# Column-group modulation with its twenty later weight chunks inside the input projection of a two-block diffusion kernel

## Chip, cores and metric

The kernel runs on one NeuronCore of one Trainium2 chip, in one launch. The metric is the device time of an execution in microseconds (us). Before the change the median of 3 runs is 4326.28 us (4324.57 to 4330.62).

## The reference, cut to what matters

Three blocks run one after the other on 512 latent rows and 256 context rows of width 1024 (block 1 is a state-space mixer, block 2 an attention, both with a mixture of experts behind them; block 3 is not touched here). The change concerns the modulation vectors of blocks 1 and 2, and where in the program they are computed.

```python
silu_c, silu_cc = silu(c), silu(c_ctx)                       # (1, 1024) and (1024,)
for i in range(2):
    sh1l, sc1l, g1l, sh2l, sc2l, g2l = split(silu_c  @ ada_w[i] + ada_b[i], 6)   # ada_w[i]: (1024, 6144)
    sh1c, sc1c, g1c, sh2c, sc2c, g2c = split(silu_cc @ ada_w[i] + ada_b[i], 6)
    h_lat = rmsnorm(x, norm1_w[i]) * (1 + sc1l) + sh1l
    h_ctx = rmsnorm(ctx, norm1_w[i]) * (1 + sc1c) + sh1c
    o_ctx, o_lat = ssd_mixer(h_ctx, h_lat, ...) if i == 0 else attn_mixer(h_ctx, h_lat, ...)
    x = x + g1l * o_lat
    x = x + g2l * moe_ec(rmsnorm(x, norm2_w[i]) * (1 + sc2l) + sh2l, ...)
# ssd_mixer begins with u @ in_w (1024 x 6208), a 5-tap convolution over the rows, and silu
```

So each `ada_w[i]` is read once (24 MB in float32) and multiplied by only two rows of conditions.

## The kernel before, in words

**Weights** come through a ring of three slots of 2 MB in SBUF (`Ring`, L72 ff.). The plan of chunks is a list made once in `build`; a chunk is a matrix of 1024 rows by 512 columns as `[128, 8, 512]`. SyncE's queue (SP) issues the loads in order: `load_to(sp, end)` issues every chunk of the plan below `end`, and ahead of chunk k waits until chunk k-3, which has its slot, is used up. A chunk is used up when its last matmul is done, or, where it is cut into two fp32r parts (high and low), when its last block is cut. SP does nothing else meanwhile: its program is one line of waits and issues.

**Stages.** Each function is a block of its own; all engines meet between two of them. In order: `setup` (masks, 20 small loads of parameter rows, their transposes, silu of the conditions), `modulation(0)`, `norm_turn` (row norm, transposes, scale and shift, fp32r parts), `ssd_project` (input projection), `ssd_scan`, `norm_turn`, `project_add`, `moe(0)`, `modulation(1)`, `norm_turn`, `project` (queries, keys, values), `qk_prepare` and the rest of block 2, then block 3.

**`modulation(layer)`** (L378 to L432) takes 12 ring chunks of `ada_w[layer]`. For each, TensorE multiplies the two condition columns (the stationary operand is 128 x 2) by 8 slices of 512 columns in float32 (L405), VectorE adds the bias (L421), and at the end 32 small transposes (L412) turn shifts and scales into per-partition columns `modc`; the rows go to DRAM for the gates.

**`ssd_project`** (L610 ff.) has three parts. GpSimd cuts every block of the weights: a cast to the high part (L127), then a subtraction for the low part (L133); it runs at most four blocks ahead of TensorE's marks.
- z: 4 chunks, each cut into 4 blocks of two k slices. For a block TensorE takes 6 token tiles x 2 k x 3 products of 512 columns (L440). ScalarE applies silu (L740), SP stores the rows (L658). PSUM banks go round by 8.
- dt: one chunk of only 64 columns, then a softplus on VectorE and ScalarE.
- x: 8 chunks, each cut into 4 blocks of 128 features; the 32 feature tiles are numbered f. For one f, TensorE takes 24 products of 512 and 24 of 256 columns, then `turn(f-1)`: 6 transposes (L708) of the feature tile before. ScalarE copies the products into a padded tile (L756), VectorE convolves (L801 and four times L805) and then files the transposes of f-1 (L791, L792), ScalarE applies silu (L763, L764). ScalarE's order is copy f, silu f, copy f+1. SP stores the filed tile.

What sets the order of the loads around the change is this loop of SP (L662 ff.):

```python
for f in range(ft):
    if f % 4 == 0:
        ring.load_to(sp, first + nz + 1 + f // 4 + SLOTS)
    if f >= 16:
        sp.wait_ge(silu, f + 1)
        ...
    if 1 <= f <= 24:
        sp.wait_ge(filed, f)
        ...
```

When SP comes to f = 4j it is thus told to load up to two chunks beyond the one that f = 4j uses. `filed` reaches f when `file(f-1)` is done, and VectorE does that after the convolution of f. `turn(f-1)` has two pairs of PSUM banks in turn, (4, 5) and (6, 7).

Of the kernel before, what the change touches and what calls it, by code (L numbers as in the profile page):

```python
# [289 lines left out]
def setup(env):  # L290

    nc, ins = env.nc, env.ins
    with Stage(env, 0) as st:
# [19 lines left out]
        @block.sync  # L313
        def _(sp):
            sp.wait_ge(masks, 1)
            for src, t, r, k in pieces:
                sp.dma_start(rows[r:r + k, t, :], src).then_inc(loaded, 16)
            sp.dma_start(env.dtb[:], ins["ssd_dt_bias"].rearrange("a b c -> a (b c)")
                         .partition_broadcast(P)).then_inc(loaded, 16)
            env.ring_.load_to(sp, SLOTS)  # L320
            sp.wait_ge(loaded, 16 * (len(pieces) + 1))
# [41 lines left out]
        @block.scalar  # L363
        def _(act):
            act.wait_ge(copied, 1)
# [11 lines left out]
def modulation(env, layer):  # L377


    ps, ring = env.ps, env.ring_  # L380
    n_chunks = 12
    with Stage(env, 0 if layer == 0 else X_END) as st:
        mod = st.sb("mod_rows", [2, 6 * D])
        bias = st.sb("ada_bias", [2, 6 * D])
        bias_in, added, turned, stored = st.sem("bias_in"), st.sem("bias_added"), st.sem("mod_turned"), st.sem("mod_stored")
        first, m0 = ring.take([1] * n_chunks)
        block = st.block()

        @block.sync
        def _(sp):  # L390
            sp.dma_start(bias, env.ins["ada_b"][layer, :].partition_broadcast(2)).then_inc(bias_in, 16)
            ring.load_to(sp, first + n_chunks + SLOTS)
            sp.wait_ge(added, n_chunks)
            sp.dma_start(env.mod_dram[layer, :, :], mod).then_inc(stored, 16)
            sp.wait_ge(stored, 16)

        @block.tensor
        def _(pe):
            for n in range(n_chunks):
                if n >= 4:  # L400
                    pe.wait_ge(added, n - 3)
                ring.wait(pe, first + n)
                w = ring.view(first + n, KD, HALF)
                for k in range(KD):
                    mm = pe.matmul(ps[0:2, n % 4, :], env.cond[:, k, :], w[:, k, :], start=k == 0, stop=k == KD - 1)  # L405
                mm.then_inc(ring.done, 1)
            pe.wait_ge(added, n_chunks)

            for q, piece in enumerate((0, 1, 3, 4)):
                for k in range(KD):  # L410
                    a = piece * D + k * P
                    tr = pe.transpose(ps[:, 4, q * 16 + 2 * k:q * 16 + 2 * k + 2], mod[:, a:a + P], env.ident[0:2, 0:2])  # L412
            tr.then_inc(turned, 1)

        @block.vector
        def _(dve):
            dve.wait_ge(bias_in, 16)
            for n in range(n_chunks):
                dve.wait_ge(ring.done, m0 + n + 1)
                s = slice(n * HALF, (n + 1) * HALF)  # L420
                dve.tensor_tensor(mod[:, s], ps[0:2, n % 4, :], bias[:, s], ALU.add).then_inc(added, 1)  # L421
            dve.wait_ge(turned, 1)
            v = ps[:, 4, 0:64].rearrange("p (q k v) -> p q v k", q=4, k=KD)

            for q in range(4):
                dve.tensor_copy(env.modc[:, q, :, :], v[:, q, :, :])
            dve.drain()
            for q, name in ((1, "norm1_w"), (3, "norm2_w")):
                a = env.col_at[name] + layer * KD
                for u in range(2):  # L430
                    dve.scalar_tensor_tensor(env.modc[:, q, u, :], env.modc[:, q, u, :], 1.0, env.cols[:, a:a + KD],
                                             ALU.add, ALU.mult)  # L432
# [179 lines left out]
def ssd_project(env, t, base):  # L612
# [5 lines left out]
    with Stage(env, base) as st:  # L618
# [20 lines left out]
        blocks, m0, b0 = ring.take_cut([marked(HALF)] * nz + [marked(2 * H)]  # L639
                                       + [[(all_k, slice(f * P, (f + 1) * P), 2) for f in range(4)]] * nx)  # L640
        first = blocks[0][0]
        views = {first + n: ring.view(first + n, KD, 2 * H if n == nz else HALF) for n in range(nz + 1 + nx)}
# [7 lines left out]
        def _(sp):  # L650
            sp.dma_start(alog[:], ins["ssd_A_log"].rearrange("a b c -> a (b c)").partition_broadcast(P)).then_inc(alog_in, 16)

            for n in range(nz):
                ring.load_to(sp, first + n + 1 + SLOTS)
# [4 lines left out]
            for f in range(ft):  # L659
                if f % 4 == 0:  # L660
                    ring.load_to(sp, first + nz + 1 + f // 4 + SLOTS)
# [5 lines left out]
                if 1 <= f <= 24:  # L667
# [5 lines left out]
                                 tm[:, q_ % 2, :].rearrange("p (t c) -> p t c", t=NT)).then_inc(tm_out[q_ % 2], 16)  # L673
            for par in range(2):
# [5 lines left out]
        def _(pe):  # L680
            for n in range(nz + 1):
                wide = HALF if n < nz else 2 * H
                for b in range(4):
# [3 lines left out]
                    for i in range(NT):  # L687
                        g = n * NT + i
                        if g >= 8 and b == 0:
                            pe.wait_ge(out, g - 7)  # L690
                        t_ = slice(i * P, (i + 1) * P)
                        for q in range(2):
                            k = 2 * b + q
                            mm = products(pe, ps[:, g % 8, 0:wide], (t.hh[:, k, t_], t.hl[:, k, t_]),
                                          (hi[:, q, :], lo[:, q, :]), k == 0, k == KD - 1)
# [2229 lines left out]
```

## Time and profile before

| What | us |
|---|---|
| median of 3 runs | 4326.28 |
| the profiled execution, its own time | 4335.98 |
| span of its instructions | 4334.2 |
| TensorE busy in it | 3661.4 |
| mean granted TensorE clock (1 is 2.4 GHz) | 0.894 |
| first and last start of the matmuls of L405 | 18.5 and 1929.7 |

The profile is of one execution. Times of instructions are given from the start of the span. Records of matmuls overlap, since the array is pipelined; how fast they follow one another is read from the starts. A float32 matmul appears as two records. "Idle before" is the time an engine stood still ahead of an instruction, with what ended it. PEld is the loading of stationary operands, SPq the issuing of loads and stores by SP.

### The profile page before, as it was taken

The numbers are of one execution on the slowest core, as the hardware profiler recorded it, in microseconds if no ns is written. First come the engines' busy times: TensorE is split into PE (matmuls) and PEld (weight loads), VectorE is DVE, ScalarE is ACT, GpSimd is POOL, SyncE is SP. The second block draws the span as 40 slices with busy tenths as digits, with TensorE's granted clock in tenths as the row PEclk, the third lists the DMA queues.
The fourth block names the chain that finished last, engine by engine and source line by source line (L and its number), as shares of the span: only waits on it lengthen the run. The fifth ranks groups of instructions, "written<-read, shape, count | busy, mean of one in ns | idle before, by whom it ended". The sixth has DMA issues, their size and how long they took to land. (4 is left out here: it accounts for less than half of the span.)

```text
span 4334.2 us, 44977 instructions
## 1 busy us (share of the span) xinstructions
PE 3661.4 (84%) x17353; PEld 2613.0 (60%) x17353; DVE 2334.1 (54%) x2935; ACT 1655.1 (38%) x2498; POOL 1495.3 (34%) x714
## 2 busy tenths in 40 slices
PE   8699979967969999888497899996943999577997
PEld 1588869963456666516366455554832666456876
DVE  0108856662169999811764999994068311213410
ACT  0211223322037777602252677774222311343222
POOL 0333323540056666502003566663300122123432
PEclk9889999988969999988798899997965599798998
DMA  8222343332079999861003899993100022122230
GB/s 283 77 102 72 124 155 98 98 127 97 11 290 381 383 386 383 313 240 41 1 1 139 323 378 377 379 378 129 57 24 0 10 88 93 58 73 88 79 125 34
DMA packets 300449, 703.78 MB, mean 162 GB/s; under 512 B 15688, under 2 KB 62628, under 8 KB 297156
## 3 DMA queue, kind: packets, MB, share of 16 engines
q1 hardware_dynamic: 294092, 679.93, 42.6%
q0 software_dynamic: 6144, 20.98, 2.3%
q8 instruction: 138, 2.26, 0.2%
q14 instruction: 75, 0.61, 0.0%
HBM read 653.59 MB, written 47.28 MB: 162 GB/s over the span
## 5 line engine op out<-in xcount | busy, mean ns | idle before, releaser
L133 POOL TENSOR_TENSOR weights_low<-ring,weights_high 128x1024 fp32r<-128x1024 f32 (+2 forms) x210 | 493.0, 2352 | 1352.9 <-ACT weights_high L126 1345.5
L440 PE MATMUL ps<-h_parts,weights_high 128*128 128x512 f32 (+2 forms) x2528 | 741.1, 379 | 30.8 <-POOL weights_low L133 30.5
L440 PEld LDWEIGHTS ps<-h_parts,weights_high 128*128 128x128 f32 (+1 forms) x2528 | 464.0, 191 | 126.3 <-POOL weights_low L133 31.5
L440 PE MATMUL ps<-h_parts,weights_low 128*128 128x512 f32 (+2 forms) x1264 | 475.3, 376 | 0.0
L1548 DVE TENSOR_TENSOR more_low<-area,more_high 128x1024 fp32r<-128x1024 f32 x192 | 330.4, 1759 | 0.0
L1515 ACT ACTIVATE weights_high<-ring 128x1024 fp32r<-128x1024 f32 x256 | 271.3, 1061 | 136.4 <-PE ps L1448 93.5
L1515 ACT ACTIVATE more_high<-area 128x1024 fp32r<-128x1024 f32 x256 | 271.8, 1062 | 85.8 <-PE ps L1448 85.8
L1548 DVE TENSOR_TENSOR weights_low<-ring,weights_high 128x1024 fp32r<-128x1024 f32 x192 | 300.1, 1616 | 2.7 <-ACT weights_high L1515 2.7
L1419 POOL TENSOR_TENSOR more_low<-area,more_high 128x1024 fp32r<-128x1024 f32 x64 | 242.7, 3792 | 110.7 <-ACT more_high L1515 110.7
L440 PE MATMUL ps<-weights_high,h_parts 128*128 128x512 f32 (+2 forms) x832 | 250.8, 385 | 21.8 <-POOL weights_low L133 21.8
L440 PEld LDWEIGHTS ps<-h_parts,weights_low 128*128 128x128 f32 (+1 forms) x1264 | 240.9, 191 | 46.6
L126 ACT ACTIVATE weights_high<-ring 128x1024 fp32r<-128x1024 f32 (+1 forms) x158 | 161.8, 1040 | 279.7 <-PE ps L440 230.3
L587 PE MATMUL ps<-identity,area 128*128 128x128 f32 x304 | 51.3, 345 | 207.6 <-DVE area L556 137.4
L1419 POOL TENSOR_TENSOR weights_low<-ring,weights_high 128x1024 fp32r<-128x1024 f32 x64 | 168.0, 2625 | 110.8 <-ACT weights_high L1515 110.8
L1446 PE MATMUL ps<-weights_high,gathered_high 128*96 128x512 f32 (+1 forms) x512 | 203.7, 398 | 2.9 <-DVE gathered_low L1554 2.9
L1447 PE MATMUL ps<-weights_low,gathered_high 128*96 128x512 f32 (+1 forms) x512 | 204.3, 399 | 0.0
L1448 PE MATMUL ps<-weights_high,gathered_low 128*96 128x512 f32 (+1 forms) x512 | 203.3, 397 | 0.0
L1446 PE MATMUL ps<-more_high,gathered_high 128*96 128x512 f32 (+1 forms) x512 | 202.8, 396 | 0.0
L1448 PE MATMUL ps<-more_high,gathered_low 128*96 128x512 f32 (+1 forms) x512 | 201.5, 394 | 0.0
L1447 PE MATMUL ps<-more_low,gathered_high 128*96 128x512 f32 (+1 forms) x512 | 201.1, 393 | 0.0
L440 PEld LDWEIGHTS ps<-weights_high,h_parts 128*128 128x128 f32 x832 | 167.6, 215 | 50.0 <-POOL weights_low L133 22.3
L405 PE MATMUL ps<-ring,conditions 128*2 128x512 f32 x384 | 170.8, 608 | 22.9 <-PEq L249 18.2
(408 smaller groups left out, 7545.9 us busy)
## 6 DMA issues: line engine op xcount, KB each, us to landing
ring<-in_moe_w SPq DMA_DIRECT2D x96, 2048.0 KB, 10.7
area<-in_moe_w SPq DMA_DIRECT2D x96, 2048.0 KB, 10.3
ring<-in_ada_w SPq DMA_DIRECT2D x24, 2048.0 KB, 7.8
ring<-in_ssd_in_w SPq DMA_DIRECT2D x12, 2048.0 KB, 8.6
ring<-in_w_in SPq DMA_DIRECT2D x11, 2048.0 KB, 7.7
ring<-in_w_ffn_in SPq DMA_DIRECT2D x10, 2048.0 KB, 7.8
area<-x_dram SPq DMA_DIRECT2D x18, 1024.0 KB, 5.0
ring<-in_ssd_out_w SPq DMA_DIRECT2D x4, 2048.0 KB, 8.6
```

The source lines that it names most:

```text
L126: return eng.activation(hi, src, ACT.Copy)
L133: pool.tensor_tensor(lo, views[k][:, ks, cols], hi, ALU.subtract).then_inc(self.low_p, 1)
L405: mm = pe.matmul(ps[0:2, n % 4, :], env.cond[:, k, :], w[:, k, :], start=k == 0, stop=k == KD - 1)
L440: mm = pe.matmul(out, a, b, start=start and n == 0, stop=stop and n == 2)
L587: tr = pe.transpose(ps[:, n % 8, j * P:(j + 1) * P], xn[:, first - t0 + j, k * P:(k + 1) * P], env.ident[:])
L1419: pool.tensor_tensor(lo(m), raw(m), hi(m), ALU.subtract).then_inc(low_p, 1)
L1446: pe.matmul(out, a, h, start=first, stop=False)
L1447: pe.matmul(out, a, l, start=False, stop=False)
L1448: return pe.matmul(out, b, h, start=False, stop=last)
L1515: act.activation(hi(m), raw(m), ACT.Copy).then_inc(high, 1)
L1548: dve.tensor_tensor(lo(m), raw(m), hi(m), ALU.subtract).then_inc(low_v, 1)
```

## The change

A class `Modulate` replaces `modulation`. It pads the two condition columns to 32 (30 zero columns), and lets the 8 k slices of a chunk go to four column groups of the array, `k % 4`: four partial sums stand in partitions 0, 32, 64 and 96 of one PSUM bank (`products`). ScalarE copies the bank to SBUF (`copy`), a float32 matmul with a matrix of ones and zeros adds the four up (`sums`), VectorE adds the bias (`add`), four small transposes (`turn`) and a copy (`file`) make the columns.

Of the 24 chunks, 4 (shift and scale of the first norm of block 1) are used in a new stage `prologue`, which also has the work of the first `norm_turn`. The other 20 are used in `ssd_project`: numbers 0 to 4 behind the z and dt chunks, numbers 5 to 19 in its x part, products in even f and sums in odd f. In the plan, two of them follow each x chunk. `modulation(1)` is gone. Rows go to banks 6 and 7, so z uses six banks and `turn(f-1)` one pair. The parameter rows are loaded from ScalarE's queue, and the rows of x and the first ring chunk by SP from the start.

```diff
@@ setup
-            sp.wait_ge(masks, 1)
-            for src, t, r, k in pieces:
-                sp.dma_start(rows[r:r + k, t, :], src).then_inc(loaded, 16)
...
+            env.ring_.load_to(sp, 1)
+            for i, s in enumerate(env.xin):
+                sp.dma_start(env.x0[:, i, :], s).then_inc(env.x0_in, 16)
             env.ring_.load_to(sp, SLOTS)
...
+            act.wait_ge(masks, 1)
+            for src, t, r, k in pieces:
+                act.dma_start(rows[r:r + k, t, :], src).then_inc(loaded, 16)
@@ Modulate
+    def start(self, sp):
+        for i, (layer, c) in enumerate(self.chunks):
+            sp.dma_start(self.rows[:, self.place(i)], self.env.ins["ada_b"][layer, c * HALF:(c + 1) * HALF]
+                         .partition_broadcast(2)).then_inc(self.bias_in, 16)
+    def prepare(self, pool):
+        pool.memset(self.cond, 0.0)
+        pool.tensor_copy(self.pick, self.env.ident[:, 0:2])
+        pool.drain()
+        pool.tensor_copy(self.cond[:, :, 0:2], self.env.cond[:])
+        for j in range(1, 4):
+            pool.tensor_tensor(self.pick, self.pick, self.env.ident[:, 32 * j:32 * j + 2], ALU.add)
+            pool.drain()
+        pool.drain().then_inc(self.ready, 1)
+    def products(self, pe, i, k):
+        env, bank = self.env, self.banks[0]
+        if i == 0:
+            pe.wait_ge(self.ready, 1)
+        else:
+            pe.wait_ge(self.copied, i)
+        env.ring_.wait(pe, k)
+        w = env.ring_.view(k, KD, HALF)
+        for q in range(KD):
+            j = 32 * (q % 4)
+            mm = pe.matmul(env.ps[j:j + 32, bank, :], self.cond[:, q, :], w[:, q, :], start=q < 4, stop=q >= 4,
+                           skip_group_check=True)
+        mm.then_inc(env.mod_used, 1)
+    def copy(self, act, i):
+        act.wait_ge(self.env.mod_used, self.m0 + i + 1)
+        if i >= 1:
+            act.wait_ge(self.summed, i)
+        act.activation(self.part, self.env.ps[:, self.banks[0], :], ACT.Copy).then_inc(self.copied, 1)
+    def sums(self, pe, i):
+        if i >= 1:
+            pe.wait_ge(self.filed, i)
+        pe.wait_ge(self.copied, i + 1)
+        pe.matmul(self.env.ps[0:2, self.banks[1], :], self.pick, self.part, start=True, stop=True).then_inc(self.summed, 1)
...
+    def store(self, sp):
+        for i, (layer, c) in enumerate(self.chunks):
+            if c // 2 in self.keep:
+                sp.wait_ge(self.added, i + 1)
+                sp.dma_start(self.env.mod_dram[layer, :, c * HALF:(c + 1) * HALF], self.rows[:, self.place(i)]).then_inc(self.stored, 16)
@@ prologue
+            for i in range(mod.n):
+                mod.products(pe, i, at[i])
+                mod.sums(pe, i)
+                mod.turn(pe, i)
+            for n in range(len(groups)):
+                turn(n)
...
+            for i in range(NT):
+                act.wait_ge(env.x0_in, 16 * NT)
+                act.drain()
+                act.activation(junk, x[:, i, :], ACT.Square, scale=float(D) ** -0.5, accum_out=ss[:, i:i + 1]).then_inc(squared, 1)
+            act.wait_ge(eps_in, 1)
+            act.activation(rstd, ss, ACT.Sqrt).then_inc(rooted, 1)
+            mod.copy(act, 0)
+            mod.copy(act, 1)
+            act.wait_ge(inverse, 1)
+            for i in range(NT):
+                act.activation(x[:, i, :], x[:, i, :], ACT.Copy, scale=rstd[:, i:i + 1]).then_inc(scaled, 1)
+            mod.copy(act, 2)
+            mod.copy(act, 3)
+            act.wait_ge(mod.filed, mod.n)
...
@@ ssd_project
+        mod = Modulate(env, st, [(0, c) for c in range(4, 12)] + [(1, c) for c in range(12)], (6, 7), keep=(2, 3, 4, 5))
+        first, at = len(ring.ends), []
+        parts = [marked(HALF)] * nz + [marked(2 * H)] + [[(all_k, slice(f * P, (f + 1) * P), 2) for f in range(4)]] * nx
+        m0, b0, blocks = ring.marks, ring.blocks_p, []
+        for n, chunk in enumerate(parts):
+            blocks += ring.take_cut([chunk])[0]
+            for i in range(n, n + 1) if n <= nz else range(2 * n - nz - 1, min(2 * n - nz + 1, mod.n)):
+                at.append(mod.end(i))
+        load = lambda sp, n: ring.load_to(sp, first + n + min(max(n, 2 * n - nz - 1), mod.n) + SLOTS)
@@ ssd_project, SP
+            mod.start(sp)
             for n in range(nz):
-                ring.load_to(sp, first + n + 1 + SLOTS)
+                load(sp, n + 1)
...
             for f in range(ft):
                 if f % 4 == 0:
-                    ring.load_to(sp, first + nz + 1 + f // 4 + SLOTS)
+                    load(sp, nz + 1 + f // 4)
...
+            mod.store(sp)
+            mod.kept(sp)
@@ ssd_project, TensorE
+                    if b == 1:
+                        mod.products(pe, n, at[n])
+                    elif b == 2:
+                        mod.sums(pe, n)
+                    elif b == 3:
+                        mod.turn(pe, n)
...
-                if f >= 2:
-                    pe.wait_ge(filed, f - 1)
-                b = 4 + 2 * (f % 2)
+                if f >= 1:
+                    pe.wait_ge(filed, f)
+                b = 4
...
                 if 1 <= f <= 24:
                     turn(f - 1)
+                n = nz + 1 + f // 2
+                if f % 2 == 0 and nz + 1 < n <= mod.n:
+                    mod.turn(pe, n - 1)
+                if n < mod.n:
+                    if f % 2 == 0:
+                        mod.products(pe, n, at[n])
+                    else:
+                        mod.sums(pe, n)
@@ ssd_project, GpSimd
+            mod.prepare(pool)
             ring.cut(pool, blocks, views)
@@ ssd_project, ScalarE, behind the silu of f
+                if f % 2 == 0 and nz + 1 + f // 2 < mod.n:
+                    mod.copy(act, nz + 1 + f // 2)
@@ build, the plan
-        chunks += halves(ins["ada_w"][0], 0, 6 * D)
+        ada = [halves(ins["ada_w"][i], 0, 6 * D) for i in range(2)]
+        chunks += ada[0][:4]
...
+        between = [[c] for c in ada[0][4:9]] + [(ada[0][9:] + ada[1])[c:c + 2] for c in range(0, 15, 2)]
+        for n, chunk in enumerate(halves(w, 0, DI) + halves(w, DI + nx, DI + nx + 2 * H) + halves(w, DI, DI + nx)):
+            chunks += [chunk] + between[n]
...
-        chunks += halves(ins["ada_w"][1], 0, 6 * D)
@@ build, the stages
-        modulation(env, 0)
...
-        norm_turn(env, b1 + NT * D, Xt, (t.hh, t.hl), [(0, NL, mc(1, 0), mc(0, 0)), (NL, NC, mc(1, 1), mc(0, 1))], load=xin)
+        prologue(env, b1 + NT * D, (t.hh, t.hl))
         ssd_project(env, t, b1)
...
-        modulation(env, 1)
```

## Rows read from the trace of the kernel before

**Rows 1.** The page's table of engines: busy us, share of the span, instructions.
```profile
PE 3661.4 (84%) x17353; PEld 2613.0 (60%) x17353; DVE 2334.1 (54%) x2935; ACT 1655.1 (38%) x2498; POOL 1495.3 (34%) x714
```

**Rows 2.** Stretch, length, busy PE, PEld, DVE, ACT, POOL; granted clock, DMA share, GB/s.
```profile
15.00:105.00 90.00, 85.73 (x196) 16.79 (x196) 8.14 (x12) 0.00 (x0) 0.00 (x0) 1.00 0.88 313
154.00:290.00 136.00, 135.57 (x579) 110.00 (x579) 0.00 (x0) 13.29 (x23) 53.97 (x37) 0.99 0.26 91
290.00:317.00 27.00, 26.69 (x144) 26.55 (x143) 0.07 (x1) 2.48 (x9) 11.21 (x9) 0.58 0.33 98
345.00:558.00 213.00, 212.28 (x1243) 186.06 (x1241) 175.56 (x160) 41.52 (x92) 79.62 (x45) 0.99 0.32 104
1845.00:1939.00 94.00, 87.87 (x224) 19.01 (x224) 9.05 (x20) 0.00 (x0) 0.00 (x0) 0.94 0.76 269
```

**Rows 3.** Timeline, x part, one feature tile (start us, us, engine, line; what ended idle time).
```profile
446.87 0.82 PE L708 MATMUL ps<-identity,area 128*128 128x128 f32 x6
...
456.05 0.87 PE L708 MATMUL ps<-identity,area 128*128 128x128 f32 x6
...
437.77 0.88 ACT L756 ACTIVATE area<-ps 128x512 f32<-128x512 f32 x2 [0.16 <-PE ps L440]
...
439.44 6.29 DVE L805 SCALAR_TENSOR_TENSOR area<-area,param_columns 128x772 f32<-128x772 f32 x4
445.65 0.68 DVE L791 COPY area<-ps 128x512 f32<-128x512 f32 x1
...
447.12 0.55 SPq L170 DMA_DIRECT2D ring<-in_ssd_in_w  x1
```

**Rows 4.** Timeline: the first cut for the input projection.
```profile
150.85 1.04 POOL L127 CAST weights_high<-ring 128x1024 fp32r<-128x1024 f32 x1 [145.45 <-POOLq L249]
```

**Rows 5.** Timeline of the opening: the parameter rows have landed, and the second stage begins.
```profile
12.91 0.88 PE L355 MATMUL ps<-identity,area 128*128 128x128 f32 x3 [12.91 <-DMA dt_bias<-in_ssd_dt_bias]
...
15.53 3.29 SPq L391 DMA_DIRECT2D area<-in_ada_b  x1
```

**Rows 6.** Timeline of the first modulation: two bias adds in succession, the store, the transposes.
```profile
83.42 0.68 DVE L421 TENSOR_TENSOR area<-ps,area 2x512 f32<-2x512 f32 x1 [6.19 <-PE ps L405]
...
90.29 0.68 DVE L421 TENSOR_TENSOR area<-ps,area 2x512 f32<-2x512 f32 x1 [6.19 <-PE ps L405]
...
104.73 0.26 SPq L394 DMA_DIRECT2D mod_rows_dram<-area  x1
...
104.76 2.45 PE L412 MATMUL ps<-identity,area 2*128 2x2 f32 x32 [0.77 <-DVE area L421]
```

**Rows 7.** Timeline around the second modulation: its first matmul, and the next stage's first work.
```profile
1844.99 1.86 PE L405 MATMUL ps<-ring,conditions 128*2 128x512 f32 x2 [18.16 <-PEq L249]
...
1939.32 1.06 ACT L514 ACTIVATE area<-area 128x1024 f32<-128x1024 f32 x1 [120.34 <-PEq L249]
```

**Rows 8.** Timeline in block 2's attention: 128 wide transposes, then matmuls in two column groups.
```profile
2199.91 1.53 PE L2038 MATMUL ps<-identity,area 128*128 128x128 f32 x12
2201.37 1.53 PE L2053 MATMUL ps<-area 128*64 128x128 f32 x24
```

**Rows 9.** The group of the weight loads of those matmuls (busy us, mean ns, idle before).
```profile
L2053 PEld LDWEIGHTS ps<-area 128*64 128x64 f32 x768 | 41.3, 137 | 5.2 <-ACT area L2085 2.9 <-issue 2.3
```

**Rows 10.** TensorE after an idle time in the x part: its transposes, and the stretch behind them.
```profile
343.20 1.54 PE L708 MATMUL ps<-identity,area 128*128 128x128 f32 x6 [7.10 <-ACTq L765]
...
344.70:354.90 10.20, 10.20 (x50) 8.68 (x49) 5.14 (x7) 1.54 (x3) 0.00 (x0) 0.80 0.13 39
```

**Rows 11.** Timeline of GpSimd in the x part, and of VectorE where GpSimd has ended.
```profile
583.60 1.04 POOL L127 CAST weights_high<-ring 128x1024 fp32r<-128x1024 f32 x1 [4.87 <-PE ps L440]
584.78 2.39 POOL L133 TENSOR_TENSOR weights_low<-ring,weights_high 128x1024 fp32r<-128x1024 f32 x1
...
601.88 4.32 DVE L805 SCALAR_TENSOR_TENSOR area<-area,param_columns 128x772 f32<-128x772 f32 x4
```

**Rows 12.** DMA issues from 150 to 640 us (count, KB each, median us to landing).
```profile
ring<-in_ssd_in_w SPq DMA_DIRECT2D x9, 2048.0 KB, 8.8
```

More of the change, by code:

```diff
@@ new lines, in prologue @@
+def prologue(env, base, hT):
+    ps, ring = env.ps, env.ring_
+    x, (hh, hl) = env.x0, hT
+    mc = lambda q, u, k: env.modc[:, q, u, k:k + 1]
+    groups = [(o, m, u, k) for o, m, u in ((0, LAT, 0), (LAT, CTX, 1)) for k in range(KD)]
+    with Stage(env, base) as st:
+        mod = Modulate(env, st, [(0, c) for c in range(4)], (4, 5))
+        whole = st.sb("features", [P, 4, HALF])
+        junk = st.sb("squares", [P, D])
+        ss, rstd = st.sb("mean_square", [P, NT]), st.sb("rstd", [P, NT])
+        squared, eps_in, rooted, inverse = st.sem("squared"), st.sem("eps_in"), st.sem("rooted"), st.sem("rstd_ready")
+        scaled, turned, out, high, low = (st.sem("rows_scaled"), st.sem("turned"), st.sem("features_out"), st.sem("high_parts"),
+                                          st.sem("low_parts"))
+        at = [mod.end(i) for i in range(mod.n)]
@@ L390, in _ @@
         def _(sp):
[L391 to L395, printed above, removed]
+            mod.start(sp)
+            ring.load_to(sp, len(ring.ends) + SLOTS)
+        @block.gpsimd
+        def _(pool):
+            mod.prepare(pool)
+            for n, (o, m, u, k) in enumerate(groups):
+                pool.wait_ge(out, n + 1)
+                pool.tensor_copy(hh[:, k, o:o + m], whole[:, n % 4, 0:m]).then_inc(high, 1)
@@ L397, in _, with turn @@
         @block.tensor
         def _(pe):
-            for n in range(n_chunks):
+            def turn(n):
+                o, m, u, k = groups[n]
                 if n >= 4:
[L401 to L413, printed above, removed]
+                    pe.wait_ge(out, n - 3)
+                pe.wait_ge(scaled, (o + m) // P)
+                for j in range(o // P, (o + m) // P):
+                    a = j * P - o
+                    tr = pe.transpose(ps[:, n % 4, a:a + P], x[:, j, k * P:(k + 1) * P], env.ident[:])
@@ new lines, in turn, with _ @@
+                tr.then_inc(turned, 1)
+            for i in range(mod.n):
[4 more added lines that the diff above has]
+                turn(n)
+        @block.scalar
+        def _(act):
+            for i in range(NT):
[12 more added lines that the diff above has]
+            act.wait_ge(mod.filed, mod.n)
+            for n, (o, m, u, k) in enumerate(groups):
+                act.wait_ge(turned, n + 1)
+                if n >= 4:
+                    act.wait_ge(low, n - 3)
+                act.activation(whole[:, n % 4, 0:m], ps[:, n % 4, 0:m], ACT.Identity, scale=mc(1, u, k), bias=mc(0, u, k)).then_inc(out, 1)
@@ L415, in _ @@
         @block.vector
         def _(dve):
[L417 to L432, printed above, removed]
+            dve.wait_ge(squared, NT)
+            dve.tensor_scalar(ss, ss, EPS, None, ALU.add).then_inc(eps_in, 1)
+            dve.wait_ge(rooted, 1)
@@ L435, in products @@
+            dve.reciprocal(rstd, rstd).then_inc(inverse, 1)
+            for i in range(mod.n):
+                mod.add(dve, i)
+                mod.file(dve, i)
+            for n, (o, m, u, k) in enumerate(groups):
+                dve.wait_ge(high, n + 1)
+                dve.tensor_tensor(hl[:, k, o:o + m], whole[:, n % 4, 0:m], hh[:, k, o:o + m], ALU.subtract).then_inc(low, 1)
 def products(pe, out, x, y, start, stop):
@@ L688, in _ @@
                         g = n * NT + i
[L689 to L690 removed]
+                        if g >= NT and b == 0:
+                            pe.wait_ge(out, g - NT + 1)
                         t_ = slice(i * P, (i + 1) * P)
@@ L734, in _ @@
             for n in range(nz):
+                mod.copy(act, n)
                 for i in range(NT):
@@ L769, in _ @@
             dve.memset(pad[:], 0.0).then_inc(pads, 1)
+            for n in range(nz + 1):
+                mod.add(dve, n)
+                mod.file(dve, n)
             dve.wait_ge(out, g0)
@@ L793, in file @@
                 dve.drain().then_inc(filed, 1)
-            n = PADW - 4
+            width = PADW - 4
             for f in range(ft):
+                n = nz + f // 2
+                if nz + 1 <= n < mod.n:
+                    if f % 2 == 0:
+                        mod.add(dve, n)
+                    else:
+                        mod.file(dve, n)
                 dve.wait_ge(out, g0 + 2 * f + 2)
```

88 lines of the change are left out of this document (63 added, 25 removed).

## The prediction

> **What bounds the kernel now.** I read the table of engines first: TensorE is busy 84% of the span [rows 1]. An average hides the stages, so the busy time by stretches comes next [rows 2]. From 15 to 105 us and from 1845 to 1939 us TensorE does only the modulation's matmuls while nothing else has work to speak of; in the z and x parts of the input projection it is busy 135.6 of 136 and 212.3 of 213 us. So both modulations can be gained whole, but what moves into the input projection meets a full TensorE. Last the timeline, for what the other engines do there: a feature tile takes 9.18 us (446.87 to 456.05) [rows 3], and ScalarE's copy, VectorE's convolution and ScalarE's silu are a second chain of the same length, since ScalarE does them in one order.
>
> **The opening.** Before, the first cut of the input projection starts at 150.85 us [rows 4]. Now the prologue stands there. The parameter rows land at 12.91 us and the next stage opens at 15.5 [rows 5]; they now share the DMA with 9 MB, for which I add 2 us: 17.5. `prepare` on GpSimd is some ten small instructions, 2.5 us: 20. ScalarE first squares six tiles at 1.06 us [rows 7] and 0.2 for reading the sum, and takes the root: 27. Then each chunk goes round: copy 0.6, sums 1.7 (two records at half clock), bias 0.7 [rows 6], transposes and handoffs 0.5, products 3.4 (at half clock), 6.9 us. The third copy stands behind six scalings of 1.06 us in ScalarE's queue. Four chunks are filed at 52. Sixteen feature groups of 0.85 and 0.63 us end at 65, and stage change and a second `prepare` bring the first cut to 69. That is **-82 us**; the bounds are -90 (no delay by the bulk loads, full clock) and -65 (both worse).
>
> **The second modulation** is gone: the row norm starts at 1845.0 instead of 1939.32 [rows 7], **-94 us**. In its place in the ring are the query and key weights, loaded behind the mixture of experts; nothing becomes late.
>
> **One chunk inside the projection.** Bias adds stand 6.87 us apart (83.42 to 90.29) for 16 records, 0.429 us each [rows 6]. No matmul in four column groups is in this trace. Bounds: one after another as now, 6.87 us; four at once, 16 x 0.429 / 4 = 1.72. The nearest row has two groups of 64 columns: 24 records of 128 columns pass in 1.53 us, 64 ns each, where full-width transposes of 128 columns take 128 ns (12 in 1.53) [rows 8]. Two groups halve it, so I let four quarter it: 1.72, and 0.5 for changing the tiling to and fro, 2.2. `sums` is two records, 0.86; `turn` is four of the 32 that took 2.45 us [rows 6], 0.3. Sum **3.4 us of TensorE per chunk**.
>
> Against this a weight load of 64 columns has 137 ns [rows 9] while its matmuls follow at 64 ns [rows 8], so loads overlap matmuls of the other column group. The Trainium skill, "TensorE: Matmul & The Clock Gate", section Part 3, says that loads overlap only where row groups differ, and column groups share all rows: by that rule the change would gain less, and the rows speak against the rule.
>
> **z and dt parts.** Five chunks x 3.4 = 17; in the dt part the clock is at 0.58 [rows 2], so its chunk costs 3 more: **+20 us**. If the wider matmuls bring the clock back up there, the 27 us of dt shrink by up to 14: low bound +6. Copy, add and file go to engines with 13 and 0 us of work in 136 [rows 2], no cost. Six banks instead of eight cost nothing either: a tile comes up again 8.5 us after its last product (136 / 96 x 6), and its silu, 0.6 us and a store's wait, is done by then. The 20 bias loads, at 0.26 us of SP's issue as for the store [rows 6], are 5 us ahead of a ring load that is needed half a chunk (17 us) later.
>
> **x part, work.** Fifteen chunks x 3.4 = 51. The first one's products fall into a wait of TensorE of 7.10 us [rows 10], -2.5, and TensorE needs about 9.0 of a tile's 9.18, so 3.5 goes into slack: **+45 us**. ScalarE's copy (0.6 per two tiles) and VectorE's add lie under TensorE's longer period, now 10.7 a tile. The single pair of banks for `turn` costs nothing while file(f-2) ends before TensorE is through tile f; if it doesn't, 0.5 a tile, up to +10.
>
> **x part, the late loads.** This is the large term. The plan is now x chunk, two modulation chunks, x chunk. At f = 4j SP is told to load up to the same place in the plan, but the three chunks that this names are now the x chunk for f = 4j itself and its two modulation chunks. Written out: the x chunk of f = 4 is number 13 of the stage's plan; the call at f = 0 stops at 12, the one at f = 4 brings 13, 14 and 15. A load that was issued eight tiles ahead is issued when it is due, seven times (f = 4, 8, to 28). SP comes to f = 4j once `filed` is 4j-1. Let TensorE end the matmuls of f = 4j-1 at T. The second half of the copy (0.88 for both) lasts to T+0.45. The convolution's first step takes 0.79 (438.65 to 439.44) and its four others 6.29 beside GpSimd's cutting [rows 3], 4.32 where GpSimd is idle [rows 11]; it is idle now, having nothing to cut: T+5.55. From the start of the filing to SP's ring load it was 1.47 us (445.65 to 447.12) [rows 3]: T+7.0. Landing 8.8 [rows 12]: T+15.8. Cast and subtraction, 583.60 to 587.17, 3.6 [rows 11]: T+19.4. TensorE has done its transposes and sums by T+1.5, so it stands for 17.9 us. It then starts at half clock: after 7.10 us of idling the six transposes took 1.54 us instead of 0.82, and the 10.2 us behind them have clock 0.80, that is 4.1 us at 1.2 GHz, 2.0 us lost [rows 3, 10]. 19.9 x 7 = **+139 us**. Bounds: landing at the 313 GB/s of the modulation [rows 2] takes 6.7 us, 17.8 a stall; VectorE as slow as beside cutting, 21.9: +125 to +153.
>
> **The end of the stage.** SP issues 16 stores at 0.26 us behind the last tile, **+5 us**, hidden by nothing.
>
> **Sum.** -82 - 94 + 20 + 45 + 139 + 5 = +33 us. The profiled execution (4335.98 us, span 4334.2) would come to 4369; it stands 9.7 above the median, so the median goes from 4326.28 to **4359 us**, slower by 0.8%. A difference under 0.2% (8.7 us) is about what a measurement cannot tell from no change.
>
> **Rivals.**
> - *The late load costs little* (ends faster). Place: SP's call at f = 4j. If the chunk is there in time, the 139 us fall away: 4220. Below 15.2 us a stall the sum turns negative. For it: the DMA moves only 104 GB/s there [rows 2]. Against it: the issue is late, not the transfer slow. 0.08.
> - *Column groups do not run four at once.* With weight loads exposed, 16 x 0.137 us [rows 9] make 2.2 us a chunk, 20 times 44: 4403. With two groups at a time, products take 3.4 + 0.5, 20 x 1.7 = 34: 4393. For it: the only row has two groups, and they may already use what operand bandwidth there is. Against: rows 8 show halving in full. 0.20.
> - *Column groups run one after another*: 6.87 a chunk, 20 x 4.7 = 94, and 7 more in the opening: 4460. Against it: rows 8. 0.08.
> - *The forecast*, 0.64. Its parts' bounds: opening -8 and +17, dt -14, stalls -14 and +14, products -0.5 each, banks +10. They will not all fall to one side: 4325 to 4395.
>
> **How the numbers follow.** The forecast and the second rival hold 0.84 together; 4316 to 4405 holds 8 in 10. Faster by over 0.2% (below 4317.6): the first rival, and a tail of the forecast with short stalls and a quicker dt part, 0.12. Within 0.2%: the same tail, 0.10. Slower: 0.78.
>
> **What would show it.** The first cut near 69 us. In the x part seven idle times of TensorE of 16 to 20 us ahead of L440, each with GpSimd waiting for the DMA of the ring, and a lower clock behind each. Three ring loads in a row in SP's queue at every fourth tile. A chunk's products in about 2 us, records 0.11 apart at full clock. Block 2's row norm right behind the reload of X. The main step is wrong if TensorE is idle in the x part for under 60 us in all; the price of a chunk is wrong if its records stand 0.2 us apart or more.

## The result, and the profile after

| | median us | runs | ratio to before (95%) |
|---|---|---|---|
| before, run beside it | 4328.45 | 4 (4324.57 to 4332.02) | 1 |
| after | 4361.83 | 4 (4358.02 to 4367.65) | 1.0081 (1.0068 to 1.0093) |

The changed kernel is 33 us slower, 0.8%. TensorE is busy for 76 us less than before, and the span is longer all the same. The page's table of engines of the kernel after answers to [rows 1]:

```profile
PE 3585.5 (82%) x17433; PEld 2593.7 (59%) x17433; DVE 2264.6 (52%) x2911; ACT 1677.3 (38%) x2523; POOL 1505.1 (34%) x742
```

To see where the time went, I set marks on each trace and compare the stretches between them. All but the last are the start of an instruction that both kernels have: the first cut of the input projection; the first copy of the x part; the last silu of the x part; the first full matmul of the scan, behind its loads (L898 before, L1074 after); the first square of block 2's norm. The last is the end of the span.

| Stretch | before, us | after, us | difference | predicted |
|---|---|---|---|---|
| to the first cut | 150.9 | 68.7 | -82.1 | -82 |
| z and dt parts | 174.1 | 193.8 | +19.7 | +20 |
| x part | 298.5 | 478.9 | +180.4 | +45 and +139 |
| end of the stage, start of the scan | 26.1 | 34.7 | +8.6 | +5 |
| scan to block 2's norm | 1289.8 | 1191.9 | -97.9 | -94 |
| the rest, work that no kernel here changes | 2394.9 | 2397.7 | +2.8 | 0 |
| span | 4334.2 | 4365.7 | +31.5 | +33 |

The rest takes 2391 to 2398 us in the ten profiles of this study, so its 2.8 us say nothing of the change.

**The opening.** The timeline of the kernel after; the columns are start, length, engine, line, operation, and in brackets the idle time before and what ended it. These lines answer to [rows 4, 5].

```profile
17.54 0.88 PE L352 MATMUL ps<-identity,area 128*128 128x128 f32 x3 [17.54 <-DMA dt_bias<-in_ssd_dt_bias]
...
20.33 1.06 ACT L543 ACTIVATE area<-area 128x1024 f32<-128x1024 f32 x1 [0.32 <-PEq L249]
...
22.25 3.64 PE L431 MATMUL ps<-ring,area 128*32 128x512 f32 x16 [3.83 <-POOLq L418]
29.05 0.58 ACT L439 ACTIVATE area<-ps 128x512 f32<-128x512 f32 x1
...
47.09 1.92 PE L431 MATMUL ps<-ring,area 128*32 128x512 f32 x16
...
68.74 1.04 POOL L127 CAST weights_high<-ring 128x1024 fp32r<-128x1024 f32 x1 [0.23 <-issue]
```

The parameter rows land at 17.54 (12.91 before), the sixteen records of a chunk take 3.64 us at first and 1.92 us later, and the first cut comes at 68.74.

**The x part.** Windows of the kernel after (stretch, length, busy PE, PEld, DVE, ACT, POOL; granted clock, DMA share, GB/s), beside [rows 2]; then the waits of TensorE and of GpSimd in the x part (us in total, times, longest).

```profile
240.00:742.00 502.00, 370.44 (x2082) 290.01 (x2081) 200.81 (x258) 74.98 (x153) 101.51 (x60) 0.85 0.34 123
72.00:240.00 168.00, 167.69 (x760) 126.24 (x760) 3.05 (x6) 18.63 (x30) 61.26 (x43) 0.95 0.40 140
```

```profile
PE ps L579 <- POOL weights_low L133: 124.8, 7, 18.7
...
POOL weights_high L127 <- DMA ring<-in_ssd_in_w: 349.5, 7, 55.5
```

In the z part TensorE has no pause. In the x part it stands still 124.8 us in 7 waits for the low part of the weights, and GpSimd, which cuts them, waits 7 times for the ring's load. One of the seven, from the last matmuls of a tile to the next tile's first ones:

```profile
297.29 0.82 PE L862 MATMUL ps<-identity,area 128*128 128x128 f32 x6
...
298.04 1.02 PE L445 MATMUL ps<-area 128*2 128x512 f32 x2
...
298.67 4.31 DVE L981 SCALAR_TENSOR_TENSOR area<-area,param_columns 128x772 f32<-128x772 f32 x4
302.89 0.69 DVE L961 COPY area<-ps 128x512 f32<-128x512 f32 x1
...
304.37 0.54 SPq L170 DMA_DIRECT2D ring<-in_ssd_in_w  x1
304.96 4.31 SPq L170 DMA_DIRECT2D ring<-in_ada_w  x2
...
312.93 1.04 POOL L127 CAST weights_high<-ring 128x1024 fp32r<-128x1024 f32 x1 [55.47 <-DMA ring<-in_ssd_in_w]
...
316.50 1.22 PE L579 MATMUL ps<-h_parts,weights_high 128*128 128x512 f32 x2 [17.44 <-POOL weights_low L133]
```

TensorE is through the products of the tile at 297.29, when its transposes start. VectorE then convolves and files, SP issues the x chunk at 304.37 and both modulation chunks behind it, GpSimd starts to cut the x chunk 8.56 us later, and its first block is cut 3.6 us after that. This is the chain that the prediction wrote out from T, with T = 297.29: SP's issue at T+7.1 (forecast T+7.0), the cut at T+15.6 (T+15.8), the matmuls at T+19.2 (T+19.4). The windows right behind this stall:

```profile
316.50:318.00 1.50, 1.50 (x4) 1.21 (x5) 0.00 (x0) 0.00 (x0) 1.36 (x2) 0.50 1.06 412
318.00:320.00 2.00, 2.00 (x6) 1.60 (x5) 0.00 (x0) 0.00 (x0) 2.00 (x2) 0.50 1.05 410
320.00:324.00 4.00, 4.00 (x16) 3.21 (x15) 0.00 (x0) 0.00 (x0) 3.85 (x3) 0.85 0.63 246
324.00:330.00 6.00, 6.00 (x52) 4.40 (x51) 2.05 (x3) 0.98 (x2) 2.83 (x2) 1.00 0.00 1
```

The granted clock is 0.50 (1.2 GHz) for 3.5 us and for 0.3 of the next 4, so 4.7 us in all, of which half, 2.4 us, is lost. In the first 8 us behind each of the seven stalls the granted clock is between 0.66 and 0.82, which by the same reckoning is 1.4 to 2.7 us a stall and 15.8 us in all.

**Behind the x part.** SP's queue of the kernel after, the stores of the modulation rows and what stands behind them; of before, the same place:

```profile
742.17 4.85 SPq L481 DMA_DIRECT2D mod_rows_dram<-area  x16
748.41 1.03 SPq L170 DMA_DIRECT2D ring<-in_ssd_out_w  x2
749.49 2.92 SPq L1029 DMA_DIRECT2D area<-x_dram  x1
```

```profile
626.63 0.38 SPq L170 DMA_DIRECT2D ring<-in_ssd_out_w  x1
627.07 0.57 SPq L853 DMA_DIRECT2D area<-x_dram  x1
```

Besides the sixteen stores there are two ring loads instead of one ahead of the scan's own loads. The scan begins with eight small matmuls and two with ones, for which all is at hand, and then waits for its loads. From the two with ones (752.50; before 631.92) to the first full one (776.06; before 649.52) it is 23.6 us instead of 17.6; I call this the scan's start.

### The profile page after: what moved, and what is told of

It is laid out like the page before. It is cut to its first block and busy times, and to the rows that moved or that the text cites. A ratio compares the mean times of both kernels' runs of the same rounds, so it can differ in the third digit from the quotient of the medians.

```text
span 4365.7 us, 45258 instructions
## 1 busy us (share of the span) xinstructions
PE 3585.5 (82%) x17433; PEld 2593.7 (59%) x17433; DVE 2264.6 (52%) x2911; ACT 1677.3 (38%) x2523; POOL 1505.1 (34%) x742
## 5 line engine op out<-in xcount | busy, mean ns | idle before, releaser
L579 PE MATMUL ps<-h_parts,weights_high 128*128 128x512 f32 (+2 forms) x2528 | 751.8, 383 | 157.4 <-POOL weights_low L133 157.4
L127 POOL CAST weights_high<-ring 128x1024 fp32r<-128x1024 f32 (+1 forms) x52 | 50.9, 979 | 463.4 <-DMA ring<-in_ssd_in_w 349.5
L726 PE MATMUL ps<-identity,area 128*128 128x128 f32 x256 | 39.6, 326 | 192.0 <-DVE area L695 125.5
```

The source lines that it names most:

```text
L127: return eng.tensor_copy(hi, src)
L579: mm = pe.matmul(out, a, b, start=start and n == 0, stop=stop and n == 2)
L726: tr = pe.transpose(ps[:, n % 8, j * P:(j + 1) * P], xn[:, first - t0 + j, k * P:(k + 1) * P], env.ident[:])
```

## Experiments

Every kernel is the changed one with one edit or two, but for one that edits the kernel before. Each is compared with the kernel before on the same chip (4327.64 us for the first four, 4325.98 us for the other four).

### The x chunk asked for one place earlier

My theory says that the seven waits come from the place in the plan up to which SP is told to load, not from the DMA. The rival is that TensorE's added work, or the traffic, makes the stretch long.

```diff
-        load = lambda sp, n: ring.load_to(sp, first + n + min(max(n, 2 * n - nz - 1), mod.n) + SLOTS)
+        load = lambda sp, n, more=0: ring.load_to(sp, first + n + min(max(n, 2 * n - nz - 1), mod.n) + SLOTS + more)
...
-                    load(sp, nz + 1 + f // 4)
+                    load(sp, nz + 1 + f // 4, 1)
```

> SP's call at every fourth tile names one more place of the plan, so the next x chunk is asked for four tiles ahead of its use. Theory (the issue of the x chunk is late, and TensorE stands 17.8 us and restarts at half clock, seven times): the 139 us go, 4362 - 139 = 4223 us, and TensorE's idle time behind GpSimd in the x part falls from 125 us to under 10. Rival (GpSimd cuts beside VectorE's convolution again, which then takes 6.3 instead of 4.3 us a tile, and this becomes the longer chain): up to 28 x 2 = 56 us come back, 4280 us. Second rival (the DMA cannot bring three chunks in four tiles): stalls stay, above 4300 us.

Measured 4293.82 us (4291.00 to 4296.90), ratio 0.9924 (0.9907 to 0.9940): 68 us less than the change, about half of what was expected. TensorE's waits in the x part, and one of the places:

```profile
PE ps L431 <- DMA ring<-in_ada_w: 50.3, 7, 7.8
```

```profile
364.15 1.55 SPq L170 DMA_DIRECT2D ring<-in_ada_w  x2
365.74 3.40 SPq L170 DMA_DIRECT2D ring<-in_ssd_in_w  x1
...
372.86 3.47 PE L431 MATMUL ps<-ring,area 128*32 128x512 f32 x16 [6.78 <-DMA ring<-in_ada_w]
...
387.05 6.91 DVE L981 SCALAR_TENSOR_TENSOR area<-area,param_columns 128x772 f32<-128x772 f32 x4
```

No wait for cut weights is left, so the x chunk is in time. What I had overlooked is the next in the plan. The first modulation chunk of the pair is used in the same tile f = 4j, and it is still issued at the same late point; in the change, the late x chunk had hidden it. Now TensorE waits for it itself, 7 times and 7.2 us on average, and its products take 3.47 us behind the wait where they take 1.92 in the change (286.92). VectorE's four steps are back at 6.91 us, since GpSimd has blocks to cut again. Both theories' numbers missed: a loading distance was at fault, but of two chunks, not of one.

### Both late chunks asked for in time

So each place in the plan is asked for as soon as the slot's last user lets it, at odd f: the chunk's predecessor by three is used up there.

```diff
-                if f % 4 == 0:
-                    load(sp, nz + 1 + f // 4)
+                if f == 0:
+                    load(sp, nz + 1)
+                elif f % 2 == 1:
+                    ring.load_to(sp, first + min(2 * (nz + 1) + 3 * (f // 4) + (5 if f % 4 == 1 else 6), len(at) + nz + 1 + nx + SLOTS))
```

> Every chunk of the x part is asked for as soon as its slot is free: behind f = 4j+1 the next x chunk and its first modulation chunk, behind f = 4j+3 its second one. In e1_early TensorE still waited 7 times, 50.3 us in all, for the modulation chunk whose products follow the first tile of an x chunk. Theory (the lateness had two parts in a row, the x chunk's and behind it the first modulation chunk's, and only both together give the whole sum): 50 us and about 10 us of clock go from 4294, 4232 us, and TensorE's idle time in the x part is under 10 us. Rival (what is left of the missing 70 us of e1_early is VectorE beside GpSimd's cutting): 4294 - 50 + 35 = 4280 us, with TensorE waiting for ScalarE's silu in every tile.

Measured 4221.58 us (4217.89 to 4226.48), ratio 0.9760 (0.9746 to 0.9773): 140 us less than the change, and faster than before. It is 10 us under my 4232. Of the 72 us to the first experiment's kernel, 5.1 lie behind the x part (24.5 us from the last silu to the scan's first full matmul instead of 29.6), where I had expected nothing. The end of dt and the x part as a window, then the x part alone, TensorE's waits in it, SP's ring loads, and TensorE's transposes of three tiles:

```profile
240.00:604.00 364.00, 359.18 (x2080) 281.70 (x2080) 241.41 (x253) 72.53 (x151) 112.12 (x60) 0.97 0.52 181
265.00:611.00 346.00, 335.28 (x1987) 260.99 (x1985) 239.13 (x250) 69.64 (x143) 104.91 (x56) 0.99 0.52 182
```

```profile
PE ps L864 <- ACTq L932: 3.5, 1, 3.5
PE ps L445 <- ACT area L439: 1.4, 1, 1.4
```

```profile
366.01 0.54 SPq L170 DMA_DIRECT2D ring<-in_ssd_in_w  x1
366.60 0.95 SPq L170 DMA_DIRECT2D ring<-in_ada_w  x1
...
391.83 0.54 SPq L170 DMA_DIRECT2D ring<-in_ada_w  x1
...
402.37 0.82 PE L864 MATMUL ps<-identity,area 128*128 128x128 f32 x6
...
413.84 0.82 PE L864 MATMUL ps<-identity,area 128*128 128x128 f32 x6
...
424.08 0.82 PE L864 MATMUL ps<-identity,area 128*128 128x128 f32 x6
```

TensorE is busy 359 of 364 us at a clock of 0.97, against 370 of 502 us at 0.85 in the change. The x part takes 346.0 us here and 478.9 in the change: the late loads cost 132.9 us there. By the rows it would be 124.8 for the standing and 15.8 for the clock behind it, 140.6. The kernel without stalls has waits of its own (4.9 us), which takes up most of the difference; the other 2.8 us stay open. The clock is no part of it: in the x part alone it is 0.99, as in [rows 2]. What is left over the kernel before, 346.0 - 298.5 = 47.5 us, is the price of fifteen chunks' work. A tile with products lasts 11.5 us (402.37 to 413.84), one with sums instead 10.2. The DMA moved 181 GB/s on average instead of 123, so it had room all along.

### The kernel before, with its x chunks asked for only when due

The other direction: if a load at the time of its use costs what I say, the kernel before must show the same stalls without any modulation in the projection.

```diff
             for n in range(nz):
-                ring.load_to(sp, first + n + 1 + SLOTS)
+                ring.load_to(sp, min(first + n + 1 + SLOTS, first + nz + 2))
...
-                    ring.load_to(sp, first + nz + 1 + f // 4 + SLOTS)
+                    ring.load_to(sp, first + nz + 1 + f // 4 + 1)
```

> The kernel before, without any of the change, but with each x chunk asked for only when its first tile is due, seven times late. Theory (a late issue alone makes the stall: convolution and filing, landing 8.8, cutting 3.6, less transposes, and 2 us of clock): 7 x 20 = 140 us, less up to 5 of slack, 4328 + 137 = 4465 us, TensorE idle 7 x 18.5 us before L440. Rival (the stall needs the two modulation chunks that now share ring and DMA): under 60 us more, below 4388.

Measured 4476.74 us (4472.14 to 4481.20), ratio 1.0345 (1.0327 to 1.0362), 149 us more than before. TensorE's waits:

```profile
PE ps L440 <- POOL weights_low L133: 131.9, 7, 20.2
PE ps L874 <- DMA area<-b_dram: 20.3, 1, 20.3
```

The same seven waits, 18.8 us on average where the change has 17.8, with no column group and no added traffic. The x part grows by 140.5 us. The second line is the small effect behind the stage: three ring loads now stand in SP's queue ahead of the scan's own, and the scan's start takes 28.5 us instead of 17.6. My 4465 was 12 us short, and this start, which I had left out, is 10.9 of them.

### Column groups undone: one group, and two

The price of a chunk rests on four groups working at once. With all eight slices in group 0 the sums stay as they are.

```diff
-            j = 32 * (q % 4)
-            mm = pe.matmul(env.ps[j:j + 32, bank, :], self.cond[:, q, :], w[:, q, :], start=q < 4, stop=q >= 4,
-                           skip_group_check=True)
+            mm = pe.matmul(env.ps[0:32, bank, :], self.cond[:, q, :], w[:, q, :], start=q == 0, stop=q == KD - 1)
...
-        act.activation(self.part, self.env.ps[:, self.banks[0], :], ACT.Copy).then_inc(self.copied, 1)
+        act.activation(self.part[0:32, :], self.env.ps[0:32, self.banks[0], :], ACT.Copy).then_inc(self.copied, 1)
...
         pool.memset(self.cond, 0.0)
+        pool.memset(self.part, 0.0)
```

> The same kernel, but all eight k slices of a chunk go to column group 0, so no two can run at once; the copy takes 32 rows. Theory (four groups run together, a chunk's products cost TensorE 2.1 us instead of 6.9, and TensorE sets the pace in z, dt and x): 20 x 4.7 = 94 us in the input projection and 10 to 18 in the opening, 4466 to 4474 us. Rival (the products lie mostly in TensorE's slack or its stalls): under 40 us more, below 4402.

With two groups, the conditions are padded to 64 columns and the matrix of ones has two rows of them:

```diff
-            j = 32 * (q % 4)
-            mm = pe.matmul(env.ps[j:j + 32, bank, :], self.cond[:, q, :], w[:, q, :], start=q < 4, stop=q >= 4,
+            j = 64 * (q % 2)
+            mm = pe.matmul(env.ps[j:j + 64, bank, :], self.cond[:, q, :], w[:, q, :], start=q < 2, stop=q >= 6,
...
-        for j in range(1, 4):
+        for j in range(2, 3):
```

> Two column groups of 64 instead of four of 32. Theory (time of the products goes with one over the number of groups): 3.6 us a chunk instead of 2.1, 20 x 1.6 = 32 us and about 5 in the opening, 4399 us. Rival (operand bandwidth limits four groups to hardly more than two): under 10 us more. Second rival (the cost is the loading of weights, 16 each time): no change.

Measured: one group 4477.89 us (4469.84 to 4486.44), ratio 1.0342 (1.0325 to 1.0359), 116 more than the change; two groups 4394.61 us (4386.29 to 4398.03), ratio 1.0153 (1.0136 to 1.0170), 33 more. The group of the products in each profile (busy us and mean ns of one; idle before, and what ended it), first of the change, then of two groups, then of one:

```profile
L431 PE MATMUL ps<-ring,area 128*32 128x512 f32 x384 | 53.0, 676 | 3.8 <-POOLq L418 3.8
```

```profile
L431 PE MATMUL ps<-ring,area 128*64 128x512 f32 x384 | 91.5, 620 | 3.4 <-POOLq L418 3.4
```

```profile
L431 PE MATMUL ps<-ring,area 128*32 128x512 f32 x384 | 174.8, 609 | 4.3 <-POOLq L419 4.3
```

For 24 chunks of 16 records that is 2.21, 3.81 and 7.28 us a chunk. The mean of one record is nearly the same in all three; it says how long a record lasts and nothing of how many run beside each other. The opening shows it without the full-width matmuls between; with one group:

```profile
22.68 9.61 PE L431 MATMUL ps<-ring,area 128*32 128x512 f32 x16 [4.29 <-POOLq L419]
35.17 7.05 PE L431 MATMUL ps<-ring,area 128*32 128x512 f32 x16
```

The second and third chunk take 7.05 us with one group (the fourth 8.75, begun at a granted clock of 0.53), the second to fourth 3.65 with two, and the fourth 1.92 with four. The 2.21 us are a mean with the opening's slow chunks in it (12.8 us for four); the twenty in the projection take 2.0 us each. The differences of the sums, 121.8 and 38.5 us, come out nearly whole in the time (116 and 33), since TensorE is full wherever it isn't waiting.

### One group, without late loads

That could still be otherwise once the stalls are gone, if something else than TensorE then set the pace. So both edits together, column groups undone and both chunks in time.

> e8_fed with all products in column group 0. Theory (TensorE sets the pace of z, dt and x, so a chunk's price adds in full with or without the late loads): the same as between the changed kernel and e2_serial, 116 us, so e8_fed + 116, about 4348 us. Rival (in the x part the chain of ScalarE and VectorE now hides some of it): + 60 to 80.

Measured 4332.82 us (10 runs, 4327.61 to 4344.14), ratio 1.0017 (1.0008 to 1.0026), 111 more than with groups where I expected 116. TensorE has no wait above 1.6 us in the x part, so it sets the pace with one group too. The two costs add up: with loads in time and one group, the change would have been worth nothing.

### The parameter rows ahead of the bulk loads

The rows landed 4.6 us later than before (17.54 for 12.91), the prediction had 2. If they set the pace of the opening, SP should let them through first.

```diff
             env.ring_.load_to(sp, 1)
+            sp.wait_ge(loaded, 16 * (len(pieces) + 1))
             for i, s in enumerate(env.xin):
```

> The changed kernel, but SP holds the rows of x and the second and third ring chunk back until the parameter rows have landed. Theory (the bulk loads delayed the parameter rows from 12.9 to 17.5 us, and ScalarE's queue of squares, root and copies sets the pace of the prologue from there): the rows land near 13.5 us but x only near 24, so the squares begin 4 us later than now; the first cut moves by 0 to +4 us, 4362 to 4366 us. Rival (the parameter rows' landing sets the pace): 4 us less, 4358 us.

Measured 4366.16 us (4361.22 to 4368.01), ratio 1.0093 (1.0077 to 1.0108), no gain.

```profile
12.10 0.88 PE L353 MATMUL ps<-identity,area 128*128 128x128 f32 x3 [12.10 <-DMA dt_bias<-in_ssd_dt_bias]
...
18.57 3.64 PE L432 MATMUL ps<-ring,area 128*32 128x512 f32 x16 [5.59 <-POOLq L419]
...
22.00 1.06 ACT L544 ACTIVATE area<-area 128x1024 f32<-128x1024 f32 x1 [7.45 <-DMA area<-in_ctx]
...
70.44 1.04 POOL L127 CAST weights_high<-ring 128x1024 fp32r<-128x1024 f32 x1 [0.23 <-issue]
```

The rows are there at 12.10 and the first products start 3.7 us earlier, but ScalarE's squares wait for the rows of x and start at 22.00 instead of 20.33, and the first copy stands behind them. The first cut moves with the squares (+1.7), not with the products. This shows that the squares set the pace of the opening from about 20 us on.

### The row stores spread over the last tiles

Last, the sixteen stores of the modulation rows one to each tile from f = 16, on top of the kernel with both chunks in time.

```diff
+                if f >= 16:
+                    mod.store_one(sp, f - 16)
-            mod.store(sp)
             mod.kept(sp)
```

> e8_fed, and the 16 stores of modulation rows are issued one by one in the last 16 tiles, not in a row behind the last. Theory (they lengthen the end of the stage by what they take of SP's queue, 3.8 us more than before the change): 4 us less than e8_fed. Rival (the stage's end is set by the last feature store's landing): no difference.

Measured 4217.22 us (4211.71 to 4221.23), ratio 0.9743 (0.9729 to 0.9756). From the last silu to the scan's first matmul it is 3.3 us instead of 7.1, as in the kernel before (3.3). The medians differ by 4.4 us, the intervals of the two ratios overlap, so the trace shows this gain and the times alone don't settle it. This is the fastest kernel of the study, 2.6% under the one before.

## Why the prediction was right

The forecast case happened, slower by a late load at every fourth tile, and the time came out 2.8 us above the number given (4361.83 against 4359). That it came so near is in part luck: the large terms were right within 4 us each, and the misses have both signs (x part -3.6, end of the stage +3.6, second modulation -3.9, the rest +2.8).

- **The opening**, -82: measured -82.1. The total was right, two of its steps were not. My 17.5 was the opening of the next stage (15.5 before, and 2 for the bulk loads), and behind it I put 2.5 us for `prepare`, so the squares at 20. In the trace the rows land only at 17.54, 4.6 us later than before and not 2; the stage opens at 20.26; and `prepare` runs beside the squares and holds up only the first products, which are done at 25.9, long before their copy. So the squares' start at 20.33 fell on my 20 by luck, since one error made up for the other. The first copy started at 29.05 where I had 27: a table load of 1.28 us stands ahead of the root, which I had left out. The rounds of the chunks then were 7.6, 7.6 and 4.9 us (copies at 29.05, 36.62, 44.22, 49.08) where I had 6.9 each; the quick last one, at full speed, made up for the late start, and the fourth was filed at 52 as written.
- **The second modulation**, -94: measured -97.9. The further 3.6 us (over 94.3, from 1844.99 to 1939.32) are scatter and no gain: 2.8 of them arise in the norm behind the scan, which takes 108.0 us in the profile before (first square to ScalarE's first copy of the projection behind it) and 105.2 after, and falls near one or the other of these in other kernels too (105.4 in the kernel before with late loads, 107.9 in the one with its stores spread).
- **A chunk's price**, 3.4 us with 2.2 for products: products measured 2.0 in the projection (2.21 over all 24), and the whole chunk 47.5 / 15 = 3.2 us in the x part. The estimate that four groups quarter the time rested on a row with two groups; the runs with one, two and four show 7.05, 3.65 and 1.92. By the rule of the Trainium skill, "TensorE: Matmul & The Clock Gate", section Part 3, that loads overlap matmuls only where row groups differ, the groups should have gained less. The runs decide against that rule for column groups: a chunk's sixteen loads have a median of 110 ns, 1.8 us in all, which cannot stand ahead of matmuls that pass in 1.92. The table of "TensorE: Matmul & The Clock Gate", section Part 3, in the Trainium skill gives 2.38 times for three column tiles of 32. No run here has three, and 2.38 lies between the 1.9 times for two and the 3.7 for four of the opening. The Trainium skill, "TensorEngine Tiling (Array Packing)", section Key Properties, has different tiles run loads and matmuls in parallel. The runs agree (7.05, 3.65 and 1.92 us).
- **z and dt**, +20: measured +19.7. **Work in the x part**, +45: 47.5, by the kernel without late loads.
- **Late loads**, +139: 132.9 in the x part. The idle time was 17.8 us a stall, forecast 17.9. The clock behind a stall cost 2.3 us on average by its windows (1.4 to 2.7), forecast 2.0. These rows alone would make 140.6; of the difference 4.9 us are waits that TensorE has without late loads too, and 2.8 stay open. That VectorE's four steps would take 4.31 us and not 6.29 while GpSimd has nothing to cut was so (298.67).
- **The end of the stage**, +5: measured +8.6, the one term clearly too small. From the last silu to the scan's first matmul it is 7.1 us instead of 3.3, and this is what the stores' issue costs, 3.8; the scan's eight small matmuls then take 1.2 us less than before (4.05 for 5.25). The other 6.0 us I had not seen: the loop's last call leaves one more ring load for the next stage, and SP issues it ahead of the scan's loads. The kernel before with late loads shows the same effect larger (10.9 us), and with all loads asked for in time the scan's start fell to 12.3 us, below the 17.6 of before. So 0, 1, 2 and 3 ring loads ahead of the scan's own go with 12.3, 17.6, 23.6 and 28.5 us.

Of the rivals, serial and paired column groups were made and measured, at 4478 and 4395 us against forecasts of 4460 and 4393. The rival that ends faster had its mechanism right and its condition false: without late loads the time is 4221.58 us (forecast 4220).

The expectation that failed by far was that of the first experiment: I had named the x chunk as the late one and not asked whether the next one in the plan was in time either.

## What to carry to other kernels

A prefetch distance counted in places of a plan is a distance in time only while every place is used up at the same pace; when chunks with other users are put between, count for each chunk how many tiles lie between its load's issue and its first use. A late load hides the next late one, so look for all of them before you mend the first. Work moved under a full engine costs its whole length there; here the move paid (2.6% with the loads in time) because the products became less than a third as long and the stages that they left had nothing else to do.

## What the runs showed that I had not expected

- The twenty small loads on ScalarE's queue landed at 17.54 us with 9 MB of bulk loads on SP's queue, at 12.10 us with only one ring chunk ahead of them.
- Four column groups in float32 take 1.92 us for what one takes 7.05. A quarter of that is 1.76, so that 0.16 us is left for changing over; I had allowed 0.5.
- In the opening the first three chunks' products take 3.64 us and the fourth's 1.92, and yet the windows have a granted clock of 1.00 throughout (20 to 40, 40 to 47 and 47 to 60 us). Behind the stalls of the x part length and granted clock go together (0.50). So in the opening the column and the lengths disagree; the lengths are what the time is made of, and why they double there no run settles.
- How many single ring loads stand in SP's queue ahead of the scan's own was worth 5 to 11 us at the start of the scan, with no change in how much was loaded.
